# Moving tiles in SBUF without touching an instruction: the matmul's moving operands at other byte offsets modulo 1024

## The chip, the core and the metric

The kernel runs on one core of one Trainium2 chip. The metric is the device time in microseconds of one execution. Before the change it is 1060.22 us, the median of three runs (1059.83 to 1062.07).

## What is computed

The reference is a stack of three transformer-like blocks on 256 tokens with 1024 features, all in float32:

- block A: RMS norm, a dilated attention (16 heads of 64, three dilation groups, so 9 x 1024 columns of QKV weights), output projection, residual; RMS norm, then a gated feed-forward network (up-projection 1024 to 2 x 2816, causal depthwise convolution of width 3, SiLU gate times value, down-projection 2816 to 1024), residual;
- block B: the same with a plain attention (at 256 tokens the block selection covers everything);
- block C: RMS norm, one input projection that feeds an 8-head attention with forget gates, a 31-wide convolution branch and a multiscale pooling branch; the three are concatenated and projected; then a third feed-forward network.

In the reference's own words the feed-forward part is

```
u = h @ w_up
uc = conv_b + sum(conv_w[j] * up[:, j:j + S] for j in range(CONV_WIDTH))
return (silu(gate) * val) @ w_down
```

## The kernel before, in words

**Split products.** Every large product is done in three TensorE matmuls on a split of both operands: a = a_hi + a_lo, w = w_hi + w_lo, and the product is hi·hi + lo·hi + hi·lo. ScalarE makes `w_hi` from `w_raw` (L362), VectorE makes `w_lo = w_raw - w_hi` (L370). The weights stream through a ring of six slots; a chunk has up to 1024 columns (4096 bytes in each partition), and 372 chunks pass.

**The activations.** `x_all` holds x transposed (8 tiles of 128 features by 256 tokens), with 16 columns of gains ahead of it, so that the first DMA brings both. `xg` is the split of x times the norm's gain: tile k has its hi part (1024 bytes) and right behind it its lo part (1024 bytes). `mix_hi`, `mix_lo` hold the split output of the attention, `g_hi[b]`, `g_lo[b]` (two buffers each, 1024 bytes) the split of the gated product in the feed-forward network; it is these four that "the gated product" in the change speaks of.

**Which operand is where in a matmul.** In a matmul one operand is loaded into the array (a weight load of 128 columns, 512 bytes in each partition), the other streams through it. Four sorts of matmul carry nearly all of the time:

- feed-forward up (L402, L404): `w_hi`, `w_lo` are loaded, `xg` streams. One matmul of L402 streams hi and lo of a tile together, 512 columns; one of L404 streams hi alone, 256 columns. They alternate, 16 in a chunk, 1056 of each;
- feed-forward down (L1707 to L1709): `w_hi`, `w_hi`, `w_lo` are loaded, `g_hi`, `g_lo`, `g_hi` stream, 256 columns each, 24 in a chunk, 1584 in all;
- output projections (L1189 to L1191): as the down-projection, with `mix_hi` and `mix_lo` streaming, 576 in all; the first projections of block C (L388 to L390) are the same with `xg` streaming, 144 in all;
- QKV (L650 to L652): here `xg` is loaded (128 tokens of it) and the weights stream, 384 columns (392 in one unit of block C), 1668 in all.

The order on each engine is written out by hand in the stage functions, and semaphores tie the engines together. Nothing of this order changes.

**Where tiles lie.** Tiles are allocated in the order in which they are declared, each at the next multiple of 32 bytes. Before the change the offsets in a partition, modulo 1024 bytes, are those in the first number column; behind the change those in the second:

| tile | before | after |
|---|---|---|
| `w_raw`, `w_hi`, `w_lo` (all slots; chunks of 128 columns then lie at 128 or 640) | 128 | 128 |
| x inside `x_all` | 192 | 128 |
| `xg` (each hi and each lo part), `mix_hi`, `mix_lo` | 192 | 128 |
| `con` | 64 | 0 |
| `ln_x`, `rms_r`, `tokbuf`, `qkT`, `v_tok`, `prob0`, `prob_t` | 96 | 768 |
| `prob1` | 608 | 256 |
| `g_hi`, `g_lo` | 256 | 928 |
| `conv_taps`, `cv_s0` | 512 | 160 |

Of the kernel before, what the change touches and what calls it, by code (L numbers as in the profile page):

```python
# [8 lines left out]
P = 128  # L9
D = 1024  # L10
TOK = 256
KT = D // P
# [27 lines left out]
WARM_UP = 16  # L40
HALVES = 3
GAINS = 16
CHUNK = KT * P
UNIT = 3 * P
QCHUNK = 2 * UNIT
# [112 lines left out]
def build(nc, x_d, xa_d, stream_d, par_d, con_d, taps_d, out_d):  # L158
# [7 lines left out]
    def sb(name, shape, dt=F32):  # L166
        return nc.alloc_sbuf_tensor(name, shape, dt)
# [5 lines left out]
    w_raw = [sb(f"w_raw{s}", [P, CHUNK]) for s in range(RING)]  # L173
    w_hi = [sb(f"w_hi{s}", [P, CHUNK], F32R) for s in range(RING)]
    w_lo = [sb(f"w_lo{s}", [P, CHUNK], F32R) for s in range(RING)]
    x_all = sb("x_all", [P, GAINS + KT * TOK])
    xT = x_all[:, GAINS:GAINS + KT * TOK].rearrange("p (k t) -> p k t", t=TOK)
    xg = sb("xg", [P, KT, 2, TOK], F32R)
    xg_hi, xg_lo = xg[:, :, 0, :], xg[:, :, 1, :]
    mix_hi = sb("mix_hi", [P, KT, TOK], F32R)  # L180
# [1 line left out]
    par = sb("par", [P, N_PAR])  # L182
    con = sb("con", [P, N_CON])
    zero = sb("zero", [P, TOK], BF16)
    ln_x = sb("ln_x", [P, TOK])
    rms_r = sb("rms_r", [P, TOK])

# [248 lines left out]
    def norm_gain(e, m):  # L436

        g = PAR_NORM + KT * e + m
        return x_all[:, m:m + 1] if e == 0 else par[:, g:g + 1]

    def first_hi_dve(eng):
        eng.wait_ge(x_first, 16)
# [1612 lines left out]
    with nc.Block() as block:  # L2055

        @block.sync
        def _(sp):
            def load(c):
                s, w = c % RING, chunk_cols(c)  # L2060
                sp.dma_start(w_raw[s][:, 0:w], stream_d[c, :, 0:w]).then_inc(w_loaded[s], 16)


            def load_half(c, kk):
                part = slice(kk * UNIT, (kk + 1) * UNIT)
                sp.dma_start(w_raw[c][:, part], stream_d[c, :, part]).then_inc(half_in[c] if kk == 0 else w_loaded[c], 16)

            def load_x(m, n, landed):
                part = slice(GAINS + m * TOK if m else 0, GAINS + (m + n) * TOK)
                sp.dma_start(x_all[:, part], xa_d[:, part]).then_inc(landed, 16)  # L2070

            load_x(0, 1, x_first)
            load_x(1, 1, x_in[0])
            for kk in range(2):
                load_half(1, kk)
            load_x(2, 2, x_in[1])
            for kk in range(2):
                load_half(2, kk)
            load(3)
            load_x(4, 2, x_in[2])  # L2080
            load(4)
            load(5)
            load_x(6, 2, x_in[3])
            sp.dma_start(con[:, 0:CON_MASKA], con_d[:, 0:CON_MASKA]).then_inc(con_in, 16)
            sp.dma_start(par[:, 0:PAR_FFN], par_d[:, 0:PAR_FFN]).then_inc(row_in, 16)
            for c in range(RING, N_CHUNKS):
                sp.wait_ge(w_lo_done, c - RING + 1)
                load(c)
                if c == RING + 10:
                    sp.dma_start(con[:, CON_MASKA:], con_d[:, CON_MASKA:]).then_inc(rest_in, 16)  # L2090
                if c == A_OUT:
                    sp.wait_ge(rest_in, 16)
                    sp.dma_start(par[:, PAR_FFN:], par_d[:, PAR_FFN:]).then_inc(rest_in, 16)
                if c == A_FFN:
                    sp.dma_start(taps[:], taps_d[:, :]).then_inc(taps_in, 16)
                if c == RING + 16:
                    sp.wait_ge(x_lo, KT)
                    sp.wait_ge(x_sq, KT)
                    for q in range(UCH):
                        sp.dma_start(xT[:, 2 * q:2 * q + 2], x_d[2 * q:2 * q + 2].rearrange("k p t -> p k t")).then_inc(x_in[q], 16)  # L2100
            for m in range(0, KT, 2):
                sp.wait_ge(x_new, 5 * KT + m + 1)
                sp.dma_start(out_d[m], xT[:, m, :]).then_inc(stored, 16)
            sp.wait_ge(stored, 16 * KT)

        @block.tensor
        def _(pe):

            pe.wait_ge(warm, 1)
            for n in range(WARM_UP):  # L2110
                nc.tensor.matmul(bank(7), zero[:, 0:P], zero[:], start=True, stop=True, skip_group_check=True)
            att_a_pe(pe)
            ffn_stage(pe, 0, ffn_pe(0))
            att_b_pe(pe)
            ffn_stage(pe, 1, ffn_pe(1))
            pre_pe(pe)
            att_c_pe(pe)
            ffn_stage(pe, 2, ffn_pe(2))

        @block.scalar  # L2120
        def _(act):
            for kk, landed in ((0, half_in[0]), (1, w_loaded[0])):
                part = slice(kk * UNIT, (kk + 1) * UNIT)
                act.dma_start(w_raw[0][:, part], stream_d[0, :, part]).then_inc(landed, 16)
            nc.scalar.preload_act_table_set("natural_log_exp_and_others")
            half_split_hi(act, 0, 0)
            half_split_hi(act, 0, 1)
            resid_act(act, 0, 1)
            half_split_hi(act, 1, 0)
            half_split_hi(act, 1, 1)  # L2130
            resid_act_sq(act, 0)
            resid_act_sq(act, 1)
            resid_act(act, 0, 2)
            half_split_hi(act, 2, 0)
            resid_act(act, 0, 3)
            half_split_hi(act, 2, 1)
            split_hi(act, 3)
            resid_act(act, 0, 4)
            resid_act(act, 0, 5)
            split_hi(act, 4)  # L2140
            split_hi(act, 5)
            resid_act(act, 0, 6)
            resid_act(act, 0, 7)
            resid_act_sq(act, 2)
            resid_act_sq(act, 3)
            att_a_act(act)
            ffn_stage(act, 0, ffn_act(0))
            nc.scalar.preload_act_table_set("natural_log_exp_and_others")
            end_act(act, 2)
            att_b_act(act)  # L2150
            ffn_stage(act, 1, ffn_act(1))
            nc.scalar.preload_act_table_set("natural_log_exp_and_others")
            end_act(act, 4)
            pre_act_f(act)
            att_c_act(act)
            ffn_stage(act, 2, ffn_act(2))
            for m in range(1, KT, 2):
                act.wait_ge(x_new, 5 * KT + m + 1)
                act.dma_start(out_d[m], xT[:, m, :]).then_inc(stored, 16)

        @block.vector
        def _(dve):
            nc.vector.memset(zero[:], 0.0).then_inc(warm, 1)
            first_hi_dve(dve)
            half_split_lo(dve, 0, 0)
            resid_dve_lo(dve, 0, 0)
            half_split_lo(dve, 0, 1)
            resid_dve_lo(dve, 0, 1)
            half_split_lo(dve, 1, 0)
            half_split_lo(dve, 1, 1)  # L2170
            resid_dve_lo(dve, 0, 2)
            half_split_lo(dve, 2, 0)
            resid_dve_lo(dve, 0, 3)
            half_split_lo(dve, 2, 1)
            split_lo(dve, 3)
            resid_dve_lo(dve, 0, 4)
            resid_dve_lo(dve, 0, 5)
            split_lo(dve, 4)
            split_lo(dve, 5)
            resid_dve_lo(dve, 0, 6)  # L2180
            resid_dve_lo(dve, 0, 7)
            gains_dve(dve)
            att_a_dve(dve)
            ffn_stage(dve, 0, ffn_dve(0))
            end_dve(dve, 2, acc, B_QKV)
            att_b_dve(dve)
            ffn_stage(dve, 1, ffn_dve(1))
            end_dve(dve, 4, acc, C_PRE)
            pre_dve_f(dve)
            att_c_dve(dve)  # L2190
            ffn_stage(dve, 2, ffn_dve(2))
            end_dve(dve, 6, acc, N_CHUNKS)

        @block.gpsimd
        def _(pool):
            nc.gpsimd.memset(cv_h[0][:], 0.0).then_inc(zeroed, 1)
            nc.gpsimd.memset(cv_h[1][:], 0.0).then_inc(zeroed, 1)
            resid_pool(pool, 0)
            tables_pool(pool)
            att_a_pool(pool)  # L2200
            resid_pool(pool, 1)
            ffn_stage(pool, 0, ffn_pool(0))
            resid_pool(pool, 2)
            att_b_pool(pool)
            resid_pool(pool, 3)
            ffn_stage(pool, 1, ffn_pool(1))
            resid_pool(pool, 4)
            pool_zeroes(pool)
            pre_pool_f(pool)
            resid_pool(pool, 5)  # L2210
            ffn_stage(pool, 2, ffn_pool(2))
# [62 lines left out]
def first_input(w):  # L2274

    x = np.zeros((P, GAINS + KT * TOK), np.float32)
    x[:, 0:KT] = w["attn_norm"][0].reshape(KT, P).T
    x[:, GAINS:] = w["x"][0].T[:, class_order()].reshape(KT, P, TOK).transpose(1, 0, 2).reshape(P, KT * TOK)
    return x
# [87 lines left out]
```

## Time and profile before

| what | value |
|---|---|
| median of three runs | 1060.22 us |
| the profiled execution | 1060.19 us |
| its span, first to last instruction | 1058.4 us |
| TensorE (matmul) busy | 1053.8 us, 100% |
| VectorE busy | 862.2 us, 81% |
| ScalarE busy | 685.9 us, 65% |
| GpSimd busy | 342.0 us, 32% |
| granted TensorE clock | 1.00 of full speed |

Each busy time is a sum over one engine. The rows of single matmuls need one remark: the recorded length of a matmul is modelled and overlaps the next one, so what a matmul costs is the distance from its start to the start of the next. In the timeline below that is the difference of the numbers in the first column, best taken over many instructions, since it is printed to 0.01 us.

### The profile page before, as it was taken

The page shows a single profiled execution, that of the slowest core. Times are in us where ns is not written, and L with a number is a line of the kernel's source. Part 1 is how long each engine was busy: PE and PEld are TensorE (multiplying, and loading weights), DVE is VectorE, ACT ScalarE, POOL GpSimd, SP SyncE. Part 2 cuts the span into 40 slices and gives each one's busy share as a digit, 9 for nine tenths or more (in the row PEclk, how much of TensorE's full clock was granted, in tenths as well). Part 3 has the DMA queues.
Part 4 walks back from the last instruction along what each step waited for, and adds up shares of the span by engine and source line. Part 5 has one row for each costly group of instructions (what it writes and reads, how often), then busy time and mean ns, then how long its engine had stood idle before and what let it go on. Part 6 is the DMA issues. An engine that isn't in the chain of part 4 may idle for free.

```text
span 1058.4 us, 21208 instructions
## 1 busy us (share of the span) xinstructions
PE 1053.8 (100%) x7508; PEld 981.7 (93%) x7508; DVE 862.2 (81%) x1588; ACT 685.9 (65%) x1262; POOL 342.0 (32%) x368
## 2 busy tenths in 40 slices
PE   9999999999999999999999999999999999999998
PEld 8999999999999999999989899999998999999998
DVE  7877778877799888887777998888896769988886
ACT  7766676776766555576776665555686666655552
POOL 4312222121365333322122553333350025533331
PEclk9999999999999999999999999999999999999999
DMA  9644545455466555535453675555434436655541
GB/s 317 225 159 150 164 151 180 149 185 196 161 219 198 195 181 190 159 110 179 152 164 120 216 216 187 188 187 189 134 112 144 146 114 225 212 187 190 183 154 41
DMA packets 57749, 183.34 MB, mean 173 GB/s; under 512 B 6352, under 2 KB 9680, under 8 KB 57424
## 3 DMA queue, kind: packets, MB, share of 16 engines
q1 hardware_dynamic: 56816, 181.52, 52.7%
q8 instruction: 41, 0.67, 0.3%
q10 hardware_dynamic: 864, 0.92, 0.3%
q14 instruction: 28, 0.23, 0.1%
HBM read 181.36 MB, written 1.05 MB: 172 GB/s over the span
## 4 chain that ended last, share of the span: by engine, by line
PE 99%; DMA 0%; DVE 0%; ACT 0%; DVEq 0%; issue 0%
PE ps L402 23%; PE ps L404 12%; PE ps L650 10%; PE ps L652 9%; PE ps L651 9%; PE ps L1707 6%; PE ps L1709 6%; PE ps L1708 6%; PE ps L1189 2%; PE ps L1191 2%; PE ps L1190 2%; PE ps L584 1%; PE ps L809 1%; PE ps L854 1%; PE ps L783 1%; PE ps L821 1%
## 5 line engine op out<-in xcount | busy, mean ns | idle before, releaser
L370 DVE TENSOR_TENSOR w_lo<-w_raw,w_hi 128x1024 fp32r<-128x1024 f32 (+2 forms) x369 | 441.0, 1210 | 56.0 <-ACT w_hi L362 55.3
L362 ACT ACTIVATE w_hi<-w_raw 128x1024 fp32r<-128x1024 f32 (+2 forms) x369 | 354.1, 972 | 163.3 <-PE ps L404 136.6
L402 PE MATMUL ps<-xg,w_hi 128*128 128x512 f32 x1056 | 374.7, 396 | 0.0
L404 PE MATMUL ps<-xg,w_lo 128*128 128x256 f32 x1056 | 297.0, 281 | 0.0
L402 PEld LDWEIGHTS ps<-xg,w_hi 128*128 128x128 f32 x1056 | 198.6, 188 | 44.6
L404 PEld LDWEIGHTS ps<-xg,w_lo 128*128 128x128 f32 x1056 | 198.1, 188 | 0.1
L1829 POOL TENSOR_TENSOR prob_t<-prob_t,qkT 128x256 f32<-128x256 f32 x63 | 100.3, 1593 | 289.6 <-ACT prob_t L1752 289.6
L650 PE MATMUL ps<-w_hi,xg 128*128 128x384 f32 (+1 forms) x556 | 193.1, 347 | 0.0
L652 PE MATMUL ps<-w_hi,xg 128*128 128x384 f32 (+1 forms) x556 | 186.8, 336 | 0.0
L651 PE MATMUL ps<-w_lo,xg 128*128 128x384 f32 (+1 forms) x556 | 186.7, 336 | 0.0
L1707 PE MATMUL ps<-g_hi,w_hi 128*128 128x256 f32 x528 | 149.2, 283 | 0.0
L1709 PE MATMUL ps<-g_hi,w_lo 128*128 128x256 f32 x528 | 148.9, 282 | 0.0
L1708 PE MATMUL ps<-g_lo,w_hi 128*128 128x256 f32 x528 | 148.6, 281 | 0.0
L1823 POOL TENSOR_TENSOR qkT<-prob,rms_r 128x256 f32<-128x256 f32 x132 | 119.2, 922 | 19.0 <-DVE prob L1766 10.3
L1799 DVE SCALAR_TENSOR_TENSOR qkT<-qkT,par 128x255 f32<-128x255 f32 (+1 forms) x264 | 111.6, 476 | 4.3 <-ACT qkT L1745 4.2
L650 PEld LDWEIGHTS ps<-w_hi,xg 128*128 128x128 f32 x556 | 104.4, 188 | 3.4 <-issue 2.7
L651 PEld LDWEIGHTS ps<-w_lo,xg 128*128 128x128 f32 x556 | 104.5, 188 | 0.1
L652 PEld LDWEIGHTS ps<-w_hi,xg 128*128 128x128 f32 x556 | 104.3, 188 | 0.0
L1707 PEld LDWEIGHTS ps<-g_hi,w_hi 128*128 128x128 f32 x528 | 99.6, 189 | 2.7
L1745 ACT ACTIVATE qkT<-qkT,par 128x256 f32<-128x256 f32 x132 | 76.4, 597 | 37.6 <-POOL qkT L1823 37.4
L1708 PEld LDWEIGHTS ps<-g_lo,w_hi 128*128 128x128 f32 x528 | 99.7, 189 | 0.0
L1709 PEld LDWEIGHTS ps<-g_hi,w_lo 128*128 128x128 f32 x528 | 99.3, 188 | 0.0
(182 smaller groups left out, 1388.5 us busy)
## 6 DMA issues: line engine op xcount, KB each, us to landing
w_raw<-w_stream SPq DMA_DIRECT2D x228, 512.0 KB, 3.6
w_raw<-w_stream SPq DMA_DIRECT2D x137, 384.0 KB, 3.4
w_raw<-w_stream SPq DMA_DIRECT2D x4, 392.0 KB, 3.0
con<-consts SPq DMA_DIRECT2D x1, 1024.0 KB, 7.5
x_all<-x_t SPq DMA_DIRECT2D x4, 256.0 KB, 5.5
conv_taps<-taps SPq DMA_DIRECT2D x1, 1024.0 KB, 7.1
w_raw<-w_stream SPq DMA_DIRECT2D x4, 192.0 KB, 4.4
x_all<-x_a SPq DMA_DIRECT2D x3, 256.0 KB, 5.5
```

The costliest lines, as they stand in the source:

```text
L362: nc.scalar.activation(w_hi[s][:, 0:w], w_raw[s][:, 0:w], ACT.Copy).then_inc(w_hi_done, 1)
L370: nc.vector.tensor_tensor(w_lo[s][:, 0:w], w_raw[s][:, 0:w], w_hi[s][:, 0:w].bitcast(F32), ALU.subtract).then_inc(w_lo_done, 1)
L402: nc.tensor.matmul(bank(b, 0, 2 * TOK), w_hi[s][:, k * P:(k + 1) * P], xg[:, k, :, :].rearrange("p h t -> p (h t)"), start=(k == 0), stop= ...
L404: last = nc.tensor.matmul(bank(b), w_lo[s][:, k * P:(k + 1) * P], xg_hi[:, k, :], start=False, stop=(k == KT - 1), skip_group_check=True)
L650: nc.tensor.matmul(out, hi, wh, start=(k == 0), stop=False)
L651: nc.tensor.matmul(out, hi, wl, start=False, stop=False)
L652: last = nc.tensor.matmul(out, lo, wh, start=False, stop=(k == KT - 1))
L1707: nc.tensor.matmul(acc(m), wh, g_hi[b][:], start=first, stop=False, skip_group_check=True)
L1708: nc.tensor.matmul(acc(m), wh, g_lo[b][:], start=False, stop=False, skip_group_check=True)
L1709: last = nc.tensor.matmul(acc(m), wl, g_hi[b][:], start=False, stop=True, skip_group_check=True)
L1799: nc.vector.scalar_tensor_tensor(cv_s[b][s][:, k:TOK], up_s[b][s][:, 0:TOK - k], par_col(f, t, per, i, 4 * s + 2 - k), cv_s[b][s][:, k:TOK ...
L1823: nc.gpsimd.tensor_tensor(up_s[t % 2][s], up_sum[s], rms_r[:], ALU.mult).then_inc(F.up, 1)
```

## The change

`x_all` gets 256 columns ahead of x in place of 16; the 16 gains move to the last 16 of these, so that DMAs still bring gains and x in one piece. Behind `zero` stands a tile of 184 floats (736 bytes) that nothing reads or writes. All tiles declared after `x_all` move up by 960 bytes, all declared after the gap by 1696 bytes. The weights' tiles, declared earlier, stay where they are. The instructions on every engine are the same ones in the same order, with the same shapes and the same waits.

```diff
+X0 = TOK
+GAP = 184
...
-    x_all = sb("x_all", [P, GAINS + KT * TOK])
-    xT = x_all[:, GAINS:GAINS + KT * TOK].rearrange("p (k t) -> p k t", t=TOK)
+    x_all = sb("x_all", [P, X0 + KT * TOK])
+    xT = x_all[:, X0:X0 + KT * TOK].rearrange("p (k t) -> p k t", t=TOK)
...
     zero = sb("zero", [P, TOK], BF16)
+    sb("gap", [P, GAP])
...
-        return x_all[:, m:m + 1] if e == 0 else par[:, g:g + 1]
+        return x_all[:, X0 - GAINS + m:X0 - GAINS + m + 1] if e == 0 else par[:, g:g + 1]
...
-                part = slice(GAINS + m * TOK if m else 0, GAINS + (m + n) * TOK)
-                sp.dma_start(x_all[:, part], xa_d[:, part]).then_inc(landed, 16)
+                a, b = GAINS + m * TOK if m else 0, GAINS + (m + n) * TOK
+                sp.dma_start(x_all[:, X0 - GAINS + a:X0 - GAINS + b], xa_d[:, a:b]).then_inc(landed, 16)
```

## Rows read from the trace of the kernel before

**Rows 1.** The page: busy engines, TensorE's granted clock, the chain that ended last
```profile
PE 1053.8 (100%) x7508; PEld 981.7 (93%) x7508; DVE 862.2 (81%) x1588; ACT 685.9 (65%) x1262; POOL 342.0 (32%) x368
...
PEclk9999999999999999999999999999999999999999
...
PE 99%; DMA 0%; DVE 0%; ACT 0%; DVEq 0%; issue 0%
```

**Rows 2.** TensorE's waits, all of them: total us, times, longest
```profile
PE ps L2111 <- DVE zero L2163: 1.1, 1, 1.1
PE ps L584 <- ACT w_hi L377: 0.4, 1, 0.4
```

**Rows 3.** The chain that ended last, by line (share of the span)
```profile
by line: PE ps L402 23.3%; PE ps L404 11.8%; PE ps L650 9.5%; PE ps L652 9.2%; PE ps L651 9.1%; PE ps L1707 5.9%; PE ps L1709 5.9%; PE ps L1708 5.9%; PE ps L1189 2.3%; PE ps L1191 2.1%; PE ps L1190 2.1%; PE ps L584 1.1%; PE ps L809 1.0%; PE
```

**Rows 4.** Output projection, a stretch of block B: start us, recorded us
```profile
553.63 0.28 PE L1189 MATMUL ps<-mix_hi,w_hi 128*128 128x256 f32 x1
...
555.89 0.28 PE L1191 MATMUL ps<-mix_hi,w_lo 128*128 128x256 f32 x1
```

**Rows 5.** Output projection, a later stretch of block B
```profile
570.42 0.28 PE L1190 MATMUL ps<-mix_lo,w_hi 128*128 128x256 f32 x1
...
576.78 0.28 PE L1190 MATMUL ps<-mix_lo,w_hi 128*128 128x256 f32 x1
```

**Rows 6.** Feed-forward down, two neighbouring chunks of block A
```profile
395.60 0.28 PE L1707 MATMUL ps<-g_hi,w_hi 128*128 128x256 f32 x1
...
398.36 0.28 PE L1709 MATMUL ps<-g_hi,w_lo 128*128 128x256 f32 x1
...
404.07 0.28 PE L1707 MATMUL ps<-g_hi,w_hi 128*128 128x256 f32 x1
...
406.79 0.28 PE L1709 MATMUL ps<-g_hi,w_lo 128*128 128x256 f32 x1
```

**Rows 7.** Feed-forward up, two stretches of block A
```profile
392.30 0.28 PE L404 MATMUL ps<-xg,w_lo 128*128 128x256 f32 x1
...
395.48 0.28 PE L404 MATMUL ps<-xg,w_lo 128*128 128x256 f32 x1
...
398.48 0.40 PE L402 MATMUL ps<-xg,w_hi 128*128 128x512 f32 x1
...
403.72 0.40 PE L402 MATMUL ps<-xg,w_hi 128*128 128x512 f32 x1
```

**Rows 8.** QKV, a stretch of block A
```profile
205.01 0.34 PE L651 MATMUL ps<-w_lo,xg 128*128 128x384 f32 x1
...
210.90 0.34 PE L652 MATMUL ps<-w_hi,xg 128*128 128x384 f32 x1
```

**Rows 9.** TensorE's groups by shape: names, columns, count | busy us, mean recorded ns
```profile
L402 PE MATMUL ps<-xg,w_hi 128*128 128x512 f32 x1056 | 374.7, 396 | 0.0
L404 PE MATMUL ps<-xg,w_lo 128*128 128x256 f32 x1056 | 297.0, 281 | 0.0
L651 PE MATMUL ps<-w_lo,xg 128*128 128x384 f32 x540 | 181.3, 336 | 0.0
L1707 PE MATMUL ps<-g_hi,w_hi 128*128 128x256 f32 x528 | 149.2, 283 | 0.0
L1708 PE MATMUL ps<-g_lo,w_hi 128*128 128x256 f32 x528 | 148.6, 281 | 0.0
L1190 PE MATMUL ps<-mix_lo,w_hi 128*128 128x256 f32 x192 | 53.5, 279 | 0.0
L389 PE MATMUL ps<-xg,w_hi 128*128 128x256 f32 x48 | 13.4, 279 | 0.0
```

**Rows 10.** Other engines' groups whose operands move: mean ns | idle before them
```profile
L1799 DVE SCALAR_TENSOR_TENSOR qkT<-qkT,par 128x255 f32<-128x255 f32 x132 | 59.6, 478 | 4.3 <-ACT qkT L1745 4.2
L1829 POOL TENSOR_TENSOR prob_t<-prob_t,qkT 128x256 f32<-128x256 f32 x63 | 100.3, 1593 | 289.6 <-ACT prob_t L1752 289.6
```

## The prediction, made before the changed kernel had run

> **What bounds the kernel now.** I read first the share of busy engines and the chain that ended last: TensorE is busy for 1053.8 of 1058.4 us, and 99% of the chain is its own [rows 1]. Then its waits: there are two, 1.5 us in all, both in the first microseconds [rows 2]. The granted clock is full in all 40 slices [rows 1], so it is TensorE's 2.4 GHz level throughout and no clock is to be won back. The kernel therefore takes as long as its matmuls take one after the other, and only the distance from start to start of matmuls can move the time. The chain by line says where it goes: feed-forward up 35.1%, QKV 27.8%, feed-forward down 17.7%, output projections 6.5% [rows 3].
>
> Then I ask of each sort how far a step is from the time of its columns. At 2.4 GHz 256 columns last 106.7 ns, 384 last 160.0 and 768 last 320.0.
>
> - Output projection, moving operand at 192 (modulo 1024), loaded weights at 128 or 640. From 553.63 to 555.89 are 20 steps: 113.0 ns each [rows 4]. From 570.42 to 576.78 are 54 steps: 117.8 ns [rows 5]. Same line, same tiles, same shape, and two speeds, each held over dozens of matmuls.
> - Feed-forward down, moving operand at 256, weights as before. From 395.60 to 398.36 are 23 steps: 120.0 ns; from 404.07 to 406.79 again 23: 118.3 ns [rows 6]. Mean 119.15.
> - Feed-forward up, `xg` at 192. A pair of L402 and L404 takes 3.18 us / 9 = 353.3 ns in one stretch and 5.24 / 15 = 349.3 ns in the next [rows 7]. Mean 351.3, so 31.3 over the columns, for two weight loads.
> - QKV, `xg` at 192 or 704 is loaded, weights at 128 or 640 stream: 5.89 us / 34 steps = 173.2 ns [rows 8].
>
> So the excess over the columns is 6.3, 11.1, 11.6, 13.3, 13.2 and (for two) 29.3 or 33.3 ns. It doesn't grow in proportion to the columns (384 have 13.2, 256 have up to 13.3), and it comes once per matmul with its weight load; it is as if the load of the next weights took a number of turns from the stream. The bottom of what is seen is about 6.5 ns, the top 13.3, one double the other. The shares of the two operand places differ as well: the shape 256 columns has recorded means of 279 with the moving operand at 192 (L1190, L389) and 281 to 283 at 256 (L1707, L1708) [rows 9]. Nothing else distinguishes L1190 from L1708: both load `w_hi` and stream 256 float columns. That is the one sign in the profile that a place in SBUF has a price, some 2 ns of 119.
>
> The Trainium skill ("TensorE: Matmul & The Clock Gate", section Step-by-step: what each phase is for) says the opposite: the stream and the weight load have a read port each, and loading the next weights takes nothing from the running matmul; its section Back-to-back issue gap gives N/2.4 + 2.5 ns, so 109.2 for 256 columns. The trace disagrees with the figure (113.0 to 120.0). By that rule no address could matter; it stands among the rivals as "no change".
>
> **The change part by part.** Working against the profiled execution, 1060.19 us (span 1058.4, 1.8 around it), within 0.03 of the median 1060.22.
>
> *Instructions:* none added, removed or moved; cost 0. *DMAs of x:* same bytes, another place, 0.
>
> *Other engines' operands* move from 96 to 768 (`prob_t`, `qkT`, `rms_r`). Whatever that does to L1799 (478 ns) or L1829 (1593 ns) [rows 10], VectorE has 19% free and GpSimd 68% [rows 1], and TensorE never waits for them [rows 2]. 0. The largest work of VectorE and ScalarE, the weights' split, reads and writes tiles that stay. Without that cover, 10% more on L1799's 264 instructions would be 12 us.
>
> *Feed-forward down* (1584 steps at 119.15, moving operand from 256 to 928). Bounds: 113.0 as in [rows 4] gives -9.7 us; one further turn of 6.7 above the 120.0 gives 126.7, +12.0 us. Between them 117.8 [rows 5] gives -2.1. The present place is the dearer of the two that the trace shows, so a new one is likelier to fall back than to rise; I take the middle of the two speeds of the other place, 115.4: 1584 x 3.75 = -5.9 us.
>
> *Feed-forward up* (1056 pairs at 351.3, stream from 192 to 128, weights at 128 or 640). Lower bound: two loads at 6.5 over 320 are 333.0, -19.3 us. Upper bound: two loads at 20, 360.0, +9.2 us. The nearest row, the better stretch held throughout (349.3), gives -2.1. I take 346.6, an excess smaller by 15%, half of the share that I give the down-projection: -5.0 us.
>
> *Output projections and L388 to L390* (576 + 144 = 720 steps, stream from 192 to 128). Mostly at 117.8. Bounds 113.0 (-3.5 us) and 120.0 (+1.6); I take 115.4: -1.7 us.
>
> *QKV* (1668 steps, 173.2; here the place of the loaded operand moves, from 192 to 128, and the stream stays). One speed alone, exactly at 13.2 over the columns. Bounds 166.5 (-11.2 us) and 179.9 (+11.2). No row shows it at any other speed; I take 0.
>
> Sum: -5.9 - 5.0 - 1.7 + 0 = -12.6. 1060.2 - 12.6 = **1047.6 us**, 1.2% faster. What becomes late next is nothing: TensorE stays the bound, and the split of the weights, 81% of VectorE, has room for 1% less time.
>
> **The rivals.**
> *The deep gain.* The new places let every matmul run at the low excess of [rows 4]. Then 9.7 + 19.3 + 3.5 + 11.2 = 43.7 us go: 1016.5; with one of the big two sorts only, 1025 to 1036. For it: 113.0 does exist, in the same kernel and the same shapes. Against: it is rare with the moving operand at 192, never held at 256, and in QKV never.
>
> *No change.* The two speeds at one address [rows 4, 5] show that address alone doesn't decide: the phase in which a stretch begins does as well. If that is all, and the 2 ns between 192 and 256 have another cause (the accumulators lie in other banks), the time stays: 1060, within 1058 to 1062.
>
> *Slower.* `xg`, `mix_hi` and `mix_lo` come to 128, which is where the weights are, so in every up, output and QKV matmul both reads begin at the same offset modulo 512. If the two reads disturb each other when they go through the same part of the memory, this is the worst place and not the best. Price: one turn more in QKV, 1668 x 6.7 = +11.2; up at 360.0, +9.2; outputs at 120.0, +1.6; down at 117.8, -2.1; together +19.9: 1080. It decides as soon as QKV's step is above 176 ns, for the gains of the down-projection (at most 9.7) can't make up for the other three. Against it: a reader of fixed pace that is one place off is disturbed just as often as one at the same place, only later; for it: no row of before has the two at the same offset.
>
> **How the numbers follow.** Forecast (a partial gain, 1036 to 1058): 0.42. Deep gain (under 1036): 0.24. No change: 0.13. Slower: 0.21, spread from 1062 to 1090. The range for 8 in 10 runs from 1026, within the deep gain, to 1066, in the lower part of the slower case; it leaves out some 8 in 100 below and 12 above. The forecast's own range is 1036 to 1058. Faster by over 0.2% (2.1 us, about what a measurement of this kernel tells from none): 0.66. Within it: 0.13. Slower: 0.21.
>
> **What would show each step right or wrong.** In the profile after, TensorE's waits must still be some 1.5 us and its chain 99%; otherwise another engine's operands mattered. Start-to-start steps: down near 115 (recorded mean of L1707 to L1709 falling from 281 to 283 to about 278), pairs of L402 and L404 near 346.6, outputs near 115, QKV unchanged at 173.2 (336 recorded for L651). QKV off 173.2 in either direction would be the largest single error, since its 1668 steps are taken as fixed though the loaded operand moves. If all steps are as before, place has no price. If the down-projection alone moves, the moving operand's place has one and x's did nothing.

## The result, and the profile after

The changed kernel takes 1055.17 us (median of six runs, 1054.99 to 1055.42). Six runs of the kernel before, the first three among them, have the median 1061.21 us; they lie in two groups, near 1060 and near 1062. The ratio is 0.9948, 95% interval 0.9938 to 0.9958: 0.5% faster, some 5.5 us, and 5.1 us below the 1060.22 from which the forecast was made. The forecast was 12.6 us. The measured time lies in the stated range and the sign is right; the size is off by a factor of more than two.

The page of the changed kernel first: busy engines, the granted clock, and the chain. They answer to [rows 1].

```profile
span 1053.2 us, 21208 instructions
...
PE 1048.7 (100%) x7508; PEld 978.6 (93%) x7508; DVE 863.9 (82%) x1588; ACT 686.6 (65%) x1262; POOL 343.0 (33%) x368
...
PEclk9999999999999999999999999999999999999999
...
PE 99%; DMA 0%; DVE 0%; ACT 0%; DVEq 0%; issue 0%
```

TensorE's busy time fell by 5.1 us and the span by 5.2; the other engines' times rose by 1.7 us or less. These are TensorE's waits in the changed kernel, which answer to [rows 2], and two groups of other engines whose operands moved, which answer to [rows 10]:

```profile
PE ps L2114 <- DVE zero L2166: 1.1, 1, 1.1
PE ps L587 <- ACT w_hi L380: 0.2, 1, 0.2
```
```profile
L1802 DVE SCALAR_TENSOR_TENSOR qkT<-qkT,par 128x255 f32<-128x255 f32 x132 | 59.7, 479 | 4.3 <-ACT qkT L1748 4.2
L1832 POOL TENSOR_TENSOR prob_t<-prob_t,qkT 128x256 f32<-128x256 f32 x63 | 101.4, 1609 | 283.0 <-ACT prob_t L1755 283.0
```

VectorE's 478 became 479 ns and GpSimd's 1593 became 1609: moving their operands did next to nothing, and nobody waited for it. So the change lies between the starts of matmuls. The timeline of the changed kernel (start in us first): a stretch of up-projection with the down-projection behind it, then outputs, then QKV.

```profile
388.94 0.39 PE L405 MATMUL ps<-xg,w_hi 128*128 128x512 f32 x1
...
394.49 0.28 PE L1710 MATMUL ps<-g_hi,w_hi 128*128 128x256 f32 x1
...
397.20 0.28 PE L1712 MATMUL ps<-g_hi,w_lo 128*128 128x256 f32 x1
...
570.01 0.28 PE L1193 MATMUL ps<-mix_lo,w_hi 128*128 128x256 f32 x1
...
574.93 0.28 PE L1192 MATMUL ps<-mix_hi,w_hi 128*128 128x256 f32 x1
...
206.15 0.33 PE L653 MATMUL ps<-w_hi,xg 128*128 128x384 f32 x1
...
210.66 0.34 PE L655 MATMUL ps<-w_hi,xg 128*128 128x384 f32 x1
```

- Up: 16 pairs in 5.55 us, 346.9 ns each, where [rows 7] had 353.3 and 349.3.
- Down: 23 steps in 2.71 us, 117.8 ns, where [rows 6] had 120.0 and 118.3.
- Outputs: 41 steps in 4.92 us, 120.0 ns, where [rows 5] had 117.8 and [rows 4] 113.0. They became slower.
- QKV: 26 steps in 4.51 us, 173.5 ns, against 173.2 in [rows 8]. The same.

The recorded means by shape agree; they answer to [rows 9] (mean ns last but one):

```profile
L405 PE MATMUL ps<-xg,w_hi 128*128 128x512 f32 x1056 | 370.3, 393 | 0.0
L407 PE MATMUL ps<-xg,w_lo 128*128 128x256 f32 x1056 | 295.7, 280 | 0.0
L1710 PE MATMUL ps<-g_hi,w_hi 128*128 128x256 f32 x528 | 148.6, 281 | 0.0
L1711 PE MATMUL ps<-g_lo,w_hi 128*128 128x256 f32 x528 | 147.8, 280 | 0.0
L1193 PE MATMUL ps<-mix_lo,w_hi 128*128 128x256 f32 x192 | 54.2, 282 | 0.0
L392 PE MATMUL ps<-xg,w_hi 128*128 128x256 f32 x48 | 13.6, 282 | 0.0
```

L1193, which streams `mix_lo`, went from 279 to 282, L392 likewise; L405 from 396 to 393.

Adding up all distances from start to start gives each sort's share of TensorE's time. The table has every full kernel of this study, in us, each from one profiled execution. "d" is the place of the operand that is no weight less the weights' place, modulo 256 bytes (why 256, the experiments show); the outputs' d is x's except in the last two rows.

| kernel | d of x | d of g | up | down | outputs | first of C | QKV | first to last matmul |
|---|---|---|---|---|---|---|---|---|
| before | 64 | 128 | 372.1 | 188.5 | 70.0 | 18.4 | 298.7 | 1053.9 |
| changed | 0 | 32 | 367.9 | 186.7 | 71.3 | 18.6 | 298.4 | 1048.6 |
| x alone | 0 | 128 | 372.7 | 188.0 | 71.4 | 18.6 | 298.6 | 1055.4 |
| g alone | 64 | 32 | 374.0 | 184.9 | 70.3 | 18.5 | 298.9 | 1052.5 |
| all at 160 | 32 | 32 | 367.7 | 185.0 | 69.9 | 18.4 | 298.4 | 1045.4 |
| x 160, g 64 | 32 | 192 | 368.4 | 186.4 | 70.0 | 18.3 | 297.9 | 1046.7 |
| changed, all 96 on | 0 | 32 | 367.7 | 186.7 | 71.3 | 18.6 | 298.2 | 1048.8 |
| g and mix at 240 | 32 | 112 | 369.5 | 182.8 | 68.7 | 18.4 | 298.3 | 1043.3 |
| the same, two views | 28 / 32 | 112 | 366.6 | 181.5 | 68.7 | 18.4 | 298.0 | 1039.4 |

### The profile page after: what moved, and what is told of

Read it like the earlier page. It is cut to its first block, busy times and chain, and to the rows that moved or that the text cites. A ratio compares the mean times of both kernels' runs of the same rounds, so it can differ in the third digit from the quotient of the medians.

```text
span 1053.2 us, 21208 instructions
## 1 busy us (share of the span) xinstructions
PE 1048.7 (100%) x7508; PEld 978.6 (93%) x7508; DVE 863.9 (82%) x1588; ACT 686.6 (65%) x1262; POOL 343.0 (33%) x368
## 4 chain that ended last, share of the span: by engine, by line
PE 99%; DMA 0%; DVE 0%; ACT 0%; DVEq 0%; issue 0%
PE ps L405 23%; PE ps L407 12%; PE ps L653 10%; PE ps L655 9%; PE ps L654 9%; PE ps L1710 6%; PE ps L1711 6%; PE ps L1712 6%; PE ps L1192 2%; PE ps L1193 2%; PE ps L1194 2%; PE ps L587 1%; PE ps L812 1%; PE ps L857 1%; PE ps L786 1%; PE ps L824 1%
## 5 line engine op out<-in xcount | busy, mean ns | idle before, releaser
L405 PE MATMUL ps<-xg,w_hi 128*128 128x512 f32 x1056 | 370.3, 393 | 0.0
L405 PEld LDWEIGHTS ps<-xg,w_hi 128*128 128x128 f32 x1056 | 197.6, 187 | 41.7
L1832 POOL TENSOR_TENSOR prob_t<-prob_t,qkT 128x256 f32<-128x256 f32 x63 | 101.4, 1609 | 283.0 <-ACT prob_t L1755 283.0
L655 PE MATMUL ps<-w_hi,xg 128*128 128x384 f32 (+1 forms) x556 | 186.4, 335 | 0.0
L1826 POOL TENSOR_TENSOR qkT<-prob,rms_r 128x256 f32<-128x256 f32 x132 | 119.6, 926 | 18.6 <-DVE prob L1769 10.2
```

The costliest lines, as they stand in the source:

```text
L405: nc.tensor.matmul(bank(b, 0, 2 * TOK), w_hi[s][:, k * P:(k + 1) * P], xg[:, k, :, :].rearrange("p h t -> p (h t)"), start=(k == 0), stop= ...
L655: last = nc.tensor.matmul(out, lo, wh, start=False, stop=(k == KT - 1))
L1826: nc.gpsimd.tensor_tensor(up_s[t % 2][s], up_sum[s], rms_r[:], ALU.mult).then_inc(F.up, 1)
```

## The experiments

My theory before them, A: each sort of matmul has a price set by the place of its own operand, and the terms add. Rival B: the phase in which a stretch begins sets it. A stretch here is a run of matmuls of one sort without another between them; its way in is what ran just before it. Further rivals came up on the way.

### x alone, and the gated product alone

The changed kernel with another gap, so that only one of the two moves:

```diff
-GAP = 184
+GAP = 16
```

That is x alone: `g_hi`, `g_lo` and `prob_t` are where they were. The next is g alone: x, `xg` and `mix` are where they were.

```diff
-X0 = TOK
-GAP = 184
+X0 = GAINS
+GAP = 168
```

> Only x, xg and mix move (x's split and mix at 128, con at 0); everything behind the gap stays where it was (g_hi and g_lo at 256, prob_t at 96). Theory A (each sort of matmul has a price that its own streamed operand's place sets, and the terms add): a pair of L405 and L407 takes 347.9 ns on the mean as in the changed kernel against 352.3, 1056 x 4.4 = -4.7 us; the output projections go to 120 ns, +1.5 us; feed-forward down stays at 119.1; together about -3.7 us, ratio 0.9965. Theory B (what a matmul costs is set by the phase in which its stretch begins, so the two moves don't add): the pairs come out elsewhere than at 347.9, or the down-projection moves off 119.1 by over 1 ns though its tiles lie where they did.

> Only the gated product and the tiles behind the gap move (g_hi and g_lo at 928, prob_t at 768); x and its split stay at 192. Theory A (prices by place, additive): feed-forward down goes from 119.1 to 118.0 ns as in the changed kernel, 1584 x 1.1 = -1.7 us, ratio 0.9984; pairs stay at 352.3 and outputs at 117.2. Theory B (phase at the beginning of a stretch): down differs from 118.0 by over 1 ns, and the pairs that follow it change too.

x alone: 1061.70 us, ratio 1.0014, interval 1.0004 to 1.0024. It is slower, if by little. g alone: 1058.91 us, ratio 0.9985 (0.9975 to 0.9994). From first to last matmul the two single effects are +1.6 and -1.4 us, 0.2 together; the two moves made together give -5.2. Theory A's sum is refuted. It had the time of g alone right (ratio 0.9984) by chance: the down-projection gained 3.5 us, twice what was expected, and the pairs, which were to stay, lost 1.9. For x alone it was right on the outputs and on the down-projection, and wrong on the pairs. The timeline of x alone shows where:

```profile
390.59 0.40 PE L405 MATMUL ps<-xg,w_hi 128*128 128x512 f32 x1
...
396.24 0.28 PE L1710 MATMUL ps<-g_hi,w_hi 128*128 128x256 f32 x1
```

16 pairs in 5.65 us are 353.1 ns, where the changed kernel has 346.9. Yet `xg` and the weights lie in both at the same addresses, and the instructions are the same. What differs for TensorE is where the matmuls in between, those of the down-projection, have their stream; other engines' tiles behind the gap have moved as well, and only a later kernel without these engines takes them out of question. With g alone the down-projection's sum is 184.9 us and in the changed kernel 186.7, again with `g_hi`, `g_lo` and the weights at identical addresses. So each sort's step seems to depend on what ran before it.

### Only TensorE, every place

To have the disputed cost by itself: a kernel that fills tiles with constants and then issues nothing but matmuls, in the three patterns, with the other operand at each of 32 places. `OFFS` holds the multiples of 32 below 1024, `REPEATS` is 2, and `marker(n)` issues n other matmuls, so that each place is entered in two ways. QKV follows in a loop of its own, entered in one way.

```
            for pattern in (down, up):
                for o in OFFS:
                    for r in range(REPEATS):
                        marker(1 + r)
                        pattern(o)
```

> Not the reference's computation: only matmuls of the three patterns on constant data, with weights fixed at 128, and the other operand at each multiple of 32 bytes modulo 1024; down-projection pattern (36 matmuls of 256 columns, twice), up-projection pattern (16 pairs of 512 and 256 columns, twice), QKV pattern (24 matmuls of 384 columns, the moved operand is the loaded one). Theory A (the place alone sets the price): the steps found in the kernels come back: down 113 or 117.8 at 192, 118.3 to 120 at 256, 118.0 at 928, 120.0 at 128; pairs 349 to 353 at 192, 346.7 at 128; QKV 173.3 at both; and at some place all patterns come near the columns' own time (106.7, 320, 160). Theory C (other engines' and the DMAs' accesses make the excess): with TensorE alone the excess over the columns nearly vanishes at all places, below 3 ns.

From its timeline, four stretches of the down pattern, two rows each: place 64 entered in one way, place 64 entered in the other, then 128, then 160.

```profile
36.86 0.28 PE L60 MATMUL ps<-arena,w_hi 128*128 128x256 f32 x1
...
40.27 0.28 PE L62 MATMUL ps<-arena,w_lo 128*128 128x256 f32 x1
...
42.22 0.28 PE L60 MATMUL ps<-arena,w_hi 128*128 128x256 f32 x1
...
44.83 0.28 PE L62 MATMUL ps<-arena,w_lo 128*128 128x256 f32 x1
...
55.08 0.28 PE L60 MATMUL ps<-arena,w_hi 128*128 128x256 f32 x1
...
58.56 0.28 PE L62 MATMUL ps<-arena,w_lo 128*128 128x256 f32 x1
...
64.37 0.28 PE L60 MATMUL ps<-arena,w_hi 128*128 128x256 f32 x1
...
67.76 0.28 PE L62 MATMUL ps<-arena,w_lo 128*128 128x256 f32 x1
```

Steps: 3.41 us / 29 = 117.6 ns and 2.61 / 23 = 113.5 at one and the same place; 3.48 / 29 = 120.0 at 128; 3.39 / 29 = 116.9 at 160. From 30 us on no other engine works there, and the queues carry 1 GB/s before the results are stored. So rival C (others' accesses) falls: the excess is TensorE's own. The 32 places gave the same eight answers four times over, with one exception (place 32 by the second way in: 118.7 the first time, 117.3 the other three), so the period is 256 bytes and not 1024. The steady steps follow in ns, with the weights at 128, each taken over whole repeats of its rhythm; where two stand, the way in decided:

| place modulo 256 | distance d | down, 256 columns | pair, 512 + 256 | QKV, 384 columns |
|---|---|---|---|---|
| 128 | 0 | 120.0 | 346.7 or 353.3 | 173.3 |
| 160 | 32 | 116.7 | 346.7 | 173.3 |
| 192 | 64 | 117.8 | 353.3 | 176.7 |
| 224 | 96 | 120.0 | 350.0 | 173.3 |
| 0 | 128 | 118.7 | 351.1 | 176.0 |
| 32 | 160 | 118.7 or 117.3 | 346.7 | 176.7 |
| 64 | 192 | 117.8 or 113.3 | 353.3 | 173.3 |
| 96 | 224 | 118.3 | 353.3 | 176.7 |

The table has the up-projection's 353.3 and the outputs' 117.8 of before, and the changed kernel's 346.7 and 120.0. It doesn't have the 113.0 of [rows 4] at the place 192, nor the kernel's QKV of 173.3 with `xg` at 192; for the latter a further run below had 173.3 and 176.7 by the way in. The last part of theory A, that some place brings all patterns near the time of their columns, did not come: the least was 113.3, 346.7 and 173.3.

### All at 160, and g at 64

If x is better at 160 than at 128, the changed kernel is not at its best:

```diff
-X0 = TOK
-GAP = 184
+X0 = TOK + 8
+GAP = 176
```

The second kernel has the same `X0` and `GAP = 152`, which puts g at 832, 64 modulo 256.

> xg and mix 32 bytes further than in the changed kernel, at 160; g_hi and g_lo stay at 928, which is 160 modulo 256. Theory D (a stream's step depends on its place modulo 256 bytes against the weights at 128, and at places with several possible rhythms on how the stretch is entered; at 160 there was one rhythm only): pairs 346.7 ns whatever went before, outputs and first projections 116.7, down 116.7. Against the changed kernel: 1056 x 1.6 = 1.7, 720 x 3.3 = 2.4, 1584 x 1.3 = 2.1, together -6.2 us: about 1049.0 us, ratio to the kernel before 0.9894. Theory E (the changed kernel's places are the best there are, 128 for x being right because the matmuls of QKV load it): as fast as the changed kernel or slower, 1055 us or more.

> As the kernel with all at 160, but g_hi and g_lo at 832, which is 64 modulo 256, the one place at which the matmuls alone had a rhythm of 113.3 ns beside one of 117.8. Theory D: the down-projection falls into one of the two; at 113.3 it gains 1584 x 3.4 = 5.4 us on the kernel with all at 160 (1043.6 us), at 117.8 it loses 1.7 us (1050.7). Nothing else changes. Theory B without places (only the phase at the beginning of a stretch counts, and any place can give any rhythm): a step other than 113.3 and 117.8.

All at 160: 1051.73 us, ratio 0.9923 (0.9907 to 0.9940), 3.4 us below the changed kernel. Down gained 1.8 us of the 2.1 expected, outputs and first of C 1.7 of 2.4, and the pairs 0.2 of 1.7 (367.7 against 367.9): the changed kernel's pairs were in the rhythm of 346.7 already, and the means of the two kernels, 348.4 and 348.2, have the first pairs of each stretch in them. So 1049.0 was missed by 2.7. With g at 64: 1053.23 us, ratio 0.9938 (0.9921 to 0.9954), where 1043.6 or 1050.7 was expected from the missed 1049.0. The down-projection took the dearer of its two rhythms, 117.7 on the mean; of its stretches of 24 and more, 59 in all, two reached 113.3. A place that has a cheap rhythm isn't enough if the way in doesn't lead there.

### Relative or absolute

> Not the reference's computation: the three patterns of matmuls alone on constant data, with the weights at 128, 160, 192 and 256 and the other operand at 8 places 32 bytes apart, each entered in three ways (behind 1, 2 or 3 other matmuls). Theory R (only the distance between the two operands modulo 256 counts): the table of steps for weights at 192 is that for weights at 128, moved on by 64 bytes. Theory S (the absolute place of the stream counts): the best places stay where they were, at 160 for the pairs, whatever the weights' place.

> The changed kernel with 96 bytes ahead of all tiles: weights at 224, x and mix at 224, g at 0, every distance as in the changed kernel. Theory R (distance to the weights alone): 1055.2 us, pairs at 348, down 118.0, outputs 120, within 0.2% of the changed kernel. Theory S (absolute places): the gain over the kernel before, 0.5%, is lost or changes by over 0.3%, as x and g lie at other places than in both kernels.

With the weights at 128, 160, 192 and 256 the steps of the matmuls alone, put by distance, are these: 0 gave 120.0 down every time; 32 gave 116.7 (two of twelve times 117.8); 192 gave 113.3 or 117.8; pairs 346.7 at 32 and 160, 353.3 at 64 and 192, at all four. Theory R holds: the distance alone sets which rhythms there are. Which of them a stretch takes is left to the way in, and here the matmuls ahead of a stretch read a tile that stayed in place. QKV at distance 64 gave 173.3, 174.7 or 176.7, by the way in.

The changed kernel, all tiles 96 bytes further:

```diff
+    sb("ahead", [P, 24])
     w_raw = [sb(f"w_raw{s}", [P, CHUNK]) for s in range(RING)]
```

1055.24 us, ratio 0.9956 (0.9940 to 0.9973), where the changed kernel has 1055.17. Every absolute place is new, and every sum of the table above is within 0.3 us of the changed kernel's. So "128 and 928" are not good places; 0 and 32 are distances.

### Four places apart, and the feed-forward network's own order

> Not the reference's computation: the down-projection's matmuls alone (24 of 256 columns) with w_hi at 128 and w_lo, g_hi and g_lo each at 8 places modulo 256, 512 combinations, and the pairs of the up-projection with w_lo at 8 places and xg at 8. Theory D: where all four lie as in the earlier table its steps come back, and no combination goes below 113.3 (an excess of 6.7 ns over the columns) or a pair below 333.3. Rival F (the excess is a clash that a right choice of four places avoids altogether): some combinations come down to 109 ns or less, and pairs to 325 or less.

Each combination of the places of `w_lo`, `g_hi` and `g_lo` ran once, entered in one way, with `w_hi` at 128; the step is the mean of the last 12 of 24. Of the 512 none was under 113.3 ns; three had it, 14 had 115.6, the dearest 122.2; 185 had 117.8. Pairs ran from 344.4 to 353.4. The excess over the columns was never under 6.7 ns, so rival F falls for the placings tried, all on the 32-byte grid.

> Not the reference's computation: on constant data, with weights at 128, the feed-forward network's own sequence of matmuls (16 pairs up, 24 down, six turns) for xg at 8 and g at 8 places modulo 256. Theory D with history (a stretch keeps the rhythm into which the end of the stretch before it drops it): for x at 128 and g at 160 pairs near 347 and down near 118, for x at 128 and g at 0 (256) pairs near 353, as in the kernels; some combination brings the down-projection to 113.3 in every turn, so that a turn is at least 24 x 4 = 0.1 us below the rest. Rival (the kernels' other work decides the entry): x at 128 gives the same pair for g at 160 and at 0.

In the timeline of this kernel, the third of six turns with x at 128 and g at 0 (start of 16 pairs, of 24 down, of the next turn), then the third with x at 128 and g at 160:

```profile
1664.11 0.39 PE L68 MATMUL ps<-arena,w_hi 128*128 128x512 f32 x1
...
1669.76 0.28 PE L60 MATMUL ps<-arena,w_hi 128*128 128x256 f32 x1
...
1672.61 0.40 PE L68 MATMUL ps<-arena,w_hi 128*128 128x512 f32 x1
...
1917.79 0.39 PE L68 MATMUL ps<-arena,w_hi 128*128 128x512 f32 x1
...
1923.34 0.28 PE L60 MATMUL ps<-arena,w_hi 128*128 128x256 f32 x1
...
1926.17 0.39 PE L68 MATMUL ps<-arena,w_hi 128*128 128x512 f32 x1
```

5.65 us / 16 = 353.1 against 5.55 / 16 = 346.9 ns a pair: the puzzle of "x alone", reproduced with TensorE alone. At distance 0 the pairs have two rhythms, and the place of the gated product decides into which of them the down-projection hands over. The other kernels come back within 2 ns a pair (pair / down, turns two to five here, the mean of the whole kernel there): for the kernel before 350.7 / 118.4 here and 352.3 / 119.0 there, for g alone 353.6 / 116.8 and 354.1 / 116.8, for x at 160 with g at 64 347.6 / 117.7 and 348.9 / 117.7. For the changed kernel the third to the fifth turn has 346.9 / 117.9, the kernel 348.4 / 117.9. The rival (other work decides the entry) is refuted for these. A rhythm need not last from turn to turn: at the changed kernel's places the first two turns had pairs at 352.2 and 352.9 before 346.9 came, and at those of before the pairs alternated between 348.6 and 352.8, much as [rows 7] has 353.3 and 349.3.

The cheapest turn is x at 128 with g at 64, 8.28 us with the down-projection at 113.6; all at 160 has 8.35, the changed kernel's places 8.38, those of before 8.45, the dearest 8.53. The expected lead of 0.1 us a turn did not come: the next placing is 0.01 us behind. The full kernel was not run with x at 128 and g at 64.

### Between the 32-byte places

> Not the reference's computation: the three patterns on constant data with weights at 128 and the other operand at every 16 bytes modulo 256, and every 4 bytes from 64 to 92 and from 128 to 156. If the step depends on the place in units of 32 bytes, each 16-byte place repeats the 32-byte place below it; if the unit is 16 bytes or less, values appear between, perhaps below 113.3 and 346.7. Places that are no multiple of 16 cost more than their neighbours if each stream is read in lines.

Places between do differ, so the unit isn't 32 bytes. At 240 (distance 112) the down pattern was at 113.3 in all three ways in; at 156 (distance 28) the pairs were at 343.3, and QKV at 180.0. Rows of these three, in this order:

```profile
232.44 0.28 PE L61 MATMUL ps<-arena,w_hi 128*128 128x256 f32 x1
...
234.93 0.28 PE L62 MATMUL ps<-arena,w_hi 128*128 128x256 f32 x1
...
891.55 0.39 PE L69 MATMUL ps<-arena,w_hi 128*128 128x512 f32 x1
...
895.67 0.39 PE L69 MATMUL ps<-arena,w_hi 128*128 128x512 f32 x1
...
1377.35 0.34 PE L82 MATMUL ps<-w_hi,arena 128*128 128x384 f32 x1
...
1379.33 0.34 PE L84 MATMUL ps<-w_hi,arena 128*128 128x384 f32 x1
```

2.49 us / 22 = 113.2 ns, 4.12 / 12 = 343.3, 1.98 / 11 = 180.0. Places off the 16-byte grid aren't dearer as such: down had 115.6 at 156 and 123.3 at 132, pairs 343.3 at 156 and 360.0 at 132 by two of three ways in. My last expectation there was wrong. The dearest down step of all was 126.7, at 136 by one way in of three.

### A version better than both

From these tables: `xg` at 160, `mix` and g at 240; then `xg` written and read 4 bytes lower, at 156, in the feed-forward networks, and at 160 in QKV. The cut below has the lines that place the tiles; `XG0` and `XG1` are the two starts of `xg`.

```diff
-    xg = sb("xg", [P, KT, 2, TOK], F32R)
+    xg_all = sb("xg", [P, KT * 2 * TOK + 64], F32R)
+    xg_at = [xg_all[:, o:o + KT * 2 * TOK].rearrange("p (k h t) -> p k h t", h=2, t=TOK) for o in (XG0, XG1)]
...
+    mix_hi, mix_lo = [m[:, MIX0:MIX0 + KT * TOK].rearrange("p (k t) -> p k t", t=TOK) for m in mix_all]
...
+    g_hi = [g_all[:, G0 + b * TOK:G0 + (b + 1) * TOK] for b in range(2)]
```

> xg at 160 modulo 256, mix_hi, mix_lo, g_hi and g_lo at 240 (slices 16 bytes off the 32-byte grid), weights at 128; no gap. Theory D with the table of the fine run: pairs 346.7 to 348, down 113.3, outputs 113.3, QKV 173.3. Against the kernel with all at 160 (1051.7 us): 1584 x 3.5 = 5.5 and 576 x 3.4 = 2.0 us less, about 1044.2 us, ratio to the kernel before 0.985. Rival (the rhythm is set by how the stretch is entered, and the loop's entries differ from the ones tried): down at 117 or above, then about 1051 us.

> As the kernel with g and mix at 240, but in the feed-forward networks xg is written and read 4 bytes lower, at 156, where the pairs alone took 343.2 ns in all three entries; in the QKV stages it stays at 160, since QKV took 180.0 ns at 156. Theory D: pairs lose 3.5 ns, 1056 x 3.5 = -3.7 us, about 1040.5 us. Rival (a 4-byte place costs ScalarE and VectorE, or the pairs find another rhythm behind the down-projection): no gain over that kernel, or a loss.

The first: 1050.14 us, ratio 0.9911 (0.9895 to 0.9928), 5.9 us above what was expected. Against all at 160 the outputs gained 1.2 us of 2.0, the down-projection 2.2 of 5.5, and the pairs lost 1.8: a chunk of 24 mostly had eleven other steps, at up to 121 ns, before it fell into 113.3. The second: 1045.82 us, ratio 0.9866 (0.9849 to 0.9882), 4.3 us below the first, of which 3.0 in the pairs and 1.2 in the down-projection, most of whose chunks now had five such steps. The gain is a little over the 3.7 expected; the 1040.5 was missed because it stood on the first kernel's 1044.2. It is the fastest of the study, 1.3% below the kernel before and 0.9% below the changed one. In its timeline 16 pairs, and the down-projection from its first and from its seventh step on:

```profile
386.61 0.39 PE L404 MATMUL ps<-xg,w_hi 128*128 128x512 f32 x1
...
392.10 0.28 PE L1709 MATMUL ps<-g_all,w_hi 128*128 128x256 f32 x1
...
392.81 0.28 PE L1709 MATMUL ps<-g_all,w_hi 128*128 128x256 f32 x1
...
394.74 0.28 PE L1711 MATMUL ps<-g_all,w_lo 128*128 128x256 f32 x1
```

That is 343.1 ns a pair, six steps of 118.3, then 17 of 113.5.

## Why the prediction was wrong, point by point

- **The bound, and the cover.** Right. TensorE alone bounds both kernels, its waits are 1.5 and 1.3 us, and other engines' operands moved at no cost.
- **Feed-forward down, -5.9 us.** Measured -1.7 (188.5 to 186.7). The step that failed is "I take the middle of the two speeds of the other place, 115.4". The matmuls fall into one of a few fixed rhythms, and a mean of two is none of them; here they came to 117.9 on the mean. The row of 117.8 [rows 5] would have given -2.1, but it is of distance 64 and this is 32, so it would have been near by luck: at the same places g alone has 116.8.
- **Output projections, -1.7 us.** Measured +1.5 with the first of C (70.0 + 18.4 to 71.3 + 18.6). The same step, with the wrong sign: at distance 0 a stream of 256 columns has one rhythm, 120.0, the upper end that I had given.
- **Feed-forward up, -5.0 us.** Measured -4.2. The value is near by luck, for its ground was wrong. 346.6 came from a share of the excess; the 346.7 is a rhythm, and at distance 0 the place of g decides whether the pairs fall into it. With x alone a pair has 353.1 and the gain is nothing.
- **QKV, 0.** Measured -0.3. Right in these kernels, though the matmuls alone had 176.7 too at the distance of before, 64, by the way in.
- **The sum.** -4.2 - 1.7 + 1.5 - 0.3 is -4.7 of the -5.2 us from first to last matmul; the rest lies in the other matmuls and in TensorE's first waits. Of the 7.4 us between -12.6 and -5.2 the middle of two speeds made 4.2 in the down-projection and 3.2 in the outputs. The form of the sum failed as well: I added independent terms, and the runs with one part each show +1.6 and -1.4 where both together make -5.2.
- **The rivals.** "Slower" had its premise half right: for the 256-column streams the same offset was as dear as any on the 32-byte grid (120.0), for QKV it was as cheap as any (173.3), and for the pairs it held both 346.7 and 353.3. "No change" had the other half: the phase at which a stretch begins does decide, among the rhythms that the distance allows. The deep gain came in none of the kernels; the best found is 1.3%.
- **The rule of the two ports.** With TensorE alone at work, the step for 256 columns went from 113.3 to 120.0 ns by the distance between the streamed and the loaded operand, and moving both together changed nothing. The Trainium skill's rule in "TensorE: Matmul & The Clock Gate", section Step-by-step: what each phase is for, that loading the next weights takes no read bandwidth from the running matmul, doesn't account for that. The 109.2 ns of the prediction were no fair test of it: the page's section Back-to-back issue gap gives its formula for the isolated gap of a matmul and says that in a stream with weight loads both operations set the spacing.

What stays open is what in TensorE or SBUF makes the period of 256 bytes. No run left the weight loads out, so that the excess comes from them is argued from the distances and not shown by itself. The 113.0 of [rows 4] is the rhythm of 113.3: in the trace of the kernel before, three of the 20 stretches of outputs with 12 matmuls or more hold it and the others 117.8, all at distance 64. The matmuls alone never had it at that distance with equal places, and which way in leads to it was not found. Other matmul shapes and data types were not tried.

## What to carry to other kernels

Where TensorE never waits, compare the distance between starts of matmuls with the time of their columns; a steady excess that differs between stretches of one shape can be such a rhythm of stream against weight load, and moving tiles by a few bytes changes it without an instruction more. Measure it with a small kernel that issues the real order of matmuls, over the distances modulo 256 bytes, since neither one sort alone nor the sum of single changes foretold it here. Between discrete outcomes take one that has been seen, never a mean of two.

## What the runs showed of the hardware

- The distance modulo 256 bytes between the streamed and the loaded operand sets which steps a float32r matmul can have: 113.3 to 120.0 ns for 256 columns on the 32-byte grid with equal places for hi and lo (122.2 with unequal ones), 346.7 to 353.3 for a pair of 512 and 256, 173.3 to 176.7 for 384. Off that grid they ran to 126.7, from 343.3 to 360.0, and to 180.0. Absolute places don't matter: 1055.24 against 1055.17 us.
- With equal places for hi and lo, a steady rhythm of one sort repeats after one to eight matmuls (after one to three pairs), and the time of a whole repeat was each time a multiple of 6.67 ns, 16 cycles at the granted 2.4 GHz: 113.3 is 17 of them, 120.0 is 18, 173.3 is 26, 346.7 is 52, three steps of 117.8 are 53, four of 116.7 are 70, five of 118.7 are 89. It is worked out from the starts in the traces; what the 16 cycles are, no run shows.
- Some distances hold two rhythms (113.3 or 117.8 at 64 and 192; 346.7 or 353.3 at 0). In the two runs on the 32-byte grid with equal places all 448 stretches were in their rhythm after at most ten matmuls and kept it to their end; with unequal places 119 of 576 found none in the 24 or 32 that they had.
- VectorE and ScalarE wrote `xg` at 156 in the feed-forward networks at no cost that could be seen: over all stages, their writes of `xg` took 654 and 506 ns on the mean, against 654 and 505 with all of them at 160, and the kernel was the fastest of all.
